# Mixture-of-experts stage: two experts share one picking matrix and one combination

## What is computed

```python
g_idx  = argmax(xf @ w_rg + b_rg)                 # one of 4 groups for each token
top_v, top_i = top_k(e_logits of that group, 2)   # two of its 8 experts
gates  = softmax(top_v) * g_gate
# each expert e works on the rows that chose it:
hdn = silu(x_e @ w1[e]) * (x_e @ w3[e])           # (rows, 1024) @ (1024, 512)
y_e = hdn @ w2[e]                                 # (rows, 512) @ (512, 1024)
out[token] = gates[token, 0] * y[slot 0] + gates[token, 1] * y[slot 1]
```

## Time and profile before

| | |
|---|---|
| Median of 3 executions | 1671.08 us (1670.26 to 1672.82) |
| The profiled execution | 1672.64 us |
| Its span, first to last instruction | 1670.8 us |
| Mean granted TensorE clock | 0.978 of 2.4 GHz |
| PE busy | 1581.0 us (95%) |
| First `hidden` of the MoE to the layer norm behind it | 178.1 to 635.8 us |

### The profile page before, as it was taken

The page is one execution under the profiler, slowest core; times in us unless marked ns, Lnnn a source line. Parts: engine busy times, 40 slices in busy tenths (PEclk is TensorE's granted clock), DMA queues, the critical chain, the costliest instruction groups (busy, mean ns, idle before and its releaser), DMA issues.

```text
span 1670.8 us, 20008 instructions
## 1 busy us (share of the span) xinstructions
PE 1581.0 (95%) x8054; PEld 1105.3 (66%) x8054; DVE 829.4 (50%) x1172; ACT 546.5 (33%) x717; POOL 61.3 (4%) x104
## 2 busy tenths in 40 slices
PE   8997999999999998999998899999999997899997
PEld 7744433333333336888897688888888886688886
DVE  1586311111111116655656766566655666576555
ACT  1251100000000003545444335444444534444442
POOL 2000000000000000000000000000000000000000
PEclk9997999999999999999989899999999998999999
DMA  9406899999999999853214359644755312179500
GB/s 312 143 1 251 349 413 429 428 428 428 428 430 428 428 407 348 277 181 125 76 51 152 123 198 367 212 132 151 264 196 169 101 59 93 51 262 353 191 0 26
DMA packets 149470, 395.20 MB, mean 237 GB/s; under 512 B 9458, under 2 KB 109936, under 8 KB 136608
## 3 DMA queue, kind: packets, MB, share of 16 engines
q1 hardware_dynamic: 146672, 385.67, 61.5%
q0 software_dynamic: 2736, 8.68, 1.4%
HBM read 393.28 MB, written 1.05 MB: 236 GB/s over the span
## 4 chain that ended last, share of the span: by engine, by line
PE 69%; DMA 15%; DVE 10%; issue 3%; ACT 3%; POOL 1%; SPq 0%; POOLq 0%; DVEq 0%; ACTq 0%
PE bank L1466 16%; DMA ring<-in_moe_w_dram 14%; PE bank L1494 12%; PE bank L1468 8%; PE bank L895 8%; PE bank L651 3%; PE bank L1481 3%; PE bank L924 2%; PE bank L704 2%; PE bank L1417 2%; PE bank L1510 1%; PE bank L912 1%; PE bank L2033 1%; PE bank L944 1%; DVE stats L546 1%
## 5 line engine op out<-in xcount | busy, mean ns | idle before, releaser
L895 PE MATMUL bank<-ring,arena 128*64 128x512 f32 x928 | 229.1, 596 | 9.8 <-DMA ring<-in_moe_w_dram 9.8
L1466 PE MATMUL bank<-x_both,split_u_hi 128*128 128x512 f32 x576 | 205.1, 399 | 0.0
L1466 PE MATMUL bank<-x_both,split_g_hi 128*128 128x512 f32 x576 | 205.0, 398 | 0.0
L895 PEld LDWEIGHTS bank<-ring,arena 128*64 128x64 f32 x928 | 68.0, 137 | 148.7 <-issue 116.0
L1468 PE MATMUL bank<-x_both,split_g_lo 128*128 128x256 f32 x576 | 161.7, 281 | 0.0
L1468 PE MATMUL bank<-x_both,split_u_lo 128*128 128x256 f32 x576 | 161.7, 281 | 0.0
L1125 DVE SCALAR_TENSOR_TENSOR arena<-arena,work 128x256 f32<-128x256 f32 x32 | 15.5, 485 | 288.8 <-PE bank L944 288.8
L1466 PEld LDWEIGHTS bank<-x_both,split_u_hi 128*128 128x128 f32 x576 | 108.2, 188 | 27.0 <-DVE split_u_lo L1283 0.3
L1466 PEld LDWEIGHTS bank<-x_both,split_g_hi 128*128 128x128 f32 x576 | 108.2, 188 | 26.4
L1283 DVE TENSOR_TENSOR split_d_lo<-ring,split_d_hi 128x2048 fp32r<-128x2048 f32 x40 | 91.7, 2292 | 58.1 <-ACT split_d_hi L1277 58.1
L1283 DVE TENSOR_TENSOR split_g_lo<-ring,split_g_hi 128x2048 fp32r<-128x2048 f32 x44 | 100.7, 2289 | 35.9 <-ACT split_g_hi L1277 35.9
(11 more groups left out here) (347 smaller groups left out, 2433.8 us busy)
## 6 DMA issues: line engine op xcount, KB each, us to landing
ring<-in_moe_w_dram SPq DMA_DIRECT2D x92, 2048.0 KB, 19.9
ring<-in_ffn_w_in_dram SPq DMA_DIRECT2D x88, 1024.0 KB, 9.3
ring<-in_ffn_w_out_dram SPq DMA_DIRECT2D x44, 1024.0 KB, 8.8
ring<-in_ml_w_in_dram SPq DMA_DIRECT2D x12, 1024.0 KB, 5.2
ring<-in_rec_w_in_dram SPq DMA_DIRECT2D x10, 1024.0 KB, 13.7
ring<-in_at_w_in_dram SPq DMA_DIRECT2D x6, 1024.0 KB, 5.2
ring<-in_rec_w_out_dram SPq DMA_DIRECT2D x5, 1024.0 KB, 9.9
gb_row<-in_ln_g_dram POOLq DMA_DIRECT2D x8, 512.0 KB, 7.0
```

What stands on the lines that cost most here:

```text
L895: i = nc.tensor.matmul(bank[4 + p][64 * j:64 * j + 64, :], xe[p][:, k, :], unit_view(n, 4)[:, k % 4, :], start=(k == 0), stop=(k == KT - 1))
L1466: nc.tensor.matmul(o[:], w_hi[:, at], x_both[:, k].rearrange("p a t -> p (a t)"), start=(k == 0), stop=False, skip_group_check=True)
```

## The change

The output rows of two experts are kept together: those of the even expert in partitions 0 to 63 of `y_2` (128 x 1024), those of the odd one in 64 to 127. `down(e)` therefore writes both halves j to partitions 64p to 64p + 63, half 0 in bank 5 and half 1 in bank 6. One picking matrix `pick_2` (128 slots x 128 tokens for each token tile) and one `combine(i)` serve experts 2i and 2i + 1; `combine` stands after the odd experts' `hidden`. `hidden` uses bank 4 for all experts. `keep` becomes two copies of 64 x 512. `down` waits for the copies of the expert before it. The second pass (overflow) is adapted in the same way, and SyncE waits for its end; that is not shown.

```diff
-        y_e = [arena[:, 9728 + i * 512:10240 + i * 512] for i in range(2)]
+        y_2 = arena[:, 9728:10752]
+        y_over = arena[:, 6144:7168]
...
+        place_2 = rt(968, NE // 2)
...
-                        i = nc.tensor.matmul(bank[4 + p][64 * j:64 * j + 64, :], xe[p][:, k, :], unit_view(n, 4)[:, k % 4, :],
+                        i = nc.tensor.matmul(bank[4][64 * j:64 * j + 64, :], xe[p][:, k, :], unit_view(n, 4)[:, k % 4, :],
...
                 pe.wait_ge(mo["hT"], e + 1)
+                if not (isinstance(e, int) and e == 0):
+                    pe.wait_ge(mo["ysb"], e)
...
-                        i = nc.tensor.matmul(bank[6][64 * j:64 * j + 64, :], hT_e[p][:, k, :],
+                        i = nc.tensor.matmul(bank[5 + j][64 * p:64 * p + 64, :], hT_e[p][:, k, :],
...
-            def combine(e, p, first=False, last=False):
+            def combine(i, first=False, last=False):
...
-                pe.wait_ge(mo["ysb"], e + 1)
-                pe.wait_ge(mo["sel"], e + 1)
+                pe.wait_ge(mo["ysb"], 2 * i + 2)
+                pe.wait_ge(mo["sel"], i + 1)
                 for t in range(TT):
                     for j in range(2):
-                        i = nc.tensor.matmul(bank[2 * t + j][:], pick_e[p][64 * j:64 * j + 64, t * P:(t + 1) * P],
-                                             y_e[p][64 * j:64 * j + 64, :], start=first, stop=last, skip_group_check=True)
+                        m = nc.tensor.matmul(bank[2 * t + j][:], pick_2[:, t * P:(t + 1) * P], y_2[:, j * HALF:(j + 1) * HALF],
+                                             start=first, stop=last, skip_group_check=True)
...
                     hidden(e, 1, 16 * (base + 2))
-                if e >= 2:
-                    combine(e - 2, e % 2, first=(e == 2))
+                    combine(0, first=True)
...
             with pe.Fori(2, NE // 2 - 1) as it:
                 for p in range(2):
                     hidden(2 * it + p, p, 16 * (it + base + p))
-                    combine(2 * it + p - 2, p)
+                    if p == 1:
+                        combine(it - 1)
                     down(2 * it + p - 1, 1 - p, 16 * (it + base + p))
                     turn(2 * it + p, p)
             hidden(NE - 2, 0, 16 * (base + NE // 2 - 1))
-            combine(NE - 4, 0)
             down(NE - 3, 1, 16 * (base + NE // 2 - 1))
             turn(NE - 2, 0)
             hidden(NE - 1, 1, 16 * (base + NE // 2), (0,))
-            combine(NE - 3, 1)
+            combine(NE // 2 - 2)
             down(NE - 2, 0, 16 * (base + NE // 2))
             hidden(NE - 1, 1, 16 * (base + NE // 2), (1,))
-            combine(NE - 2, 0)
             turn(NE - 1, 1)
             down(NE - 1, 1, 16 * (base + NE // 2))
...
-            combine(NE - 1, 1, last=True)
+            combine(NE // 2 - 1, last=True)
...
+            for p in range(2):
+                own.did(nc.vector.tensor_copy(place_2[64 * p:64 * p + 64, :], place[64 * p:64 * p + 64, 0, p::2]))
...
+            def pair_select(i, first=False):
                 if not first:
-                    dve.wait_ge(mo["comb"], e - 1)
-                select(e, p)
-                dve.wait_ge(own_sel, 2 * e + 2)
-                select_sum(p, mo["sel"])
+                    dve.wait_ge(mo["comb"], i)
+                select(pick_2, place_2[:, i:i + 1] if first else place_2[:, bass.ds(i, 1)])
+                dve.wait_ge(own_sel, 2 * i + 2)
+                nc.vector.tensor_tensor(pick_2, pick_2, sel_tmp, ALU.add).then_inc(mo["sel"], 1)
...
             with dve.Fori(1, NE // 2) as it:
                 for p in range(2):
                     expert(2 * it + p, p)
+                pair_select(it)
...
+            def keep(e, p, pair):
+
                 act.wait_ge(mo["y"], e + 1)
-                if not first:
-                    act.wait_ge(mo["comb"], e - 1)
-                nc.scalar.activation(y_e[p], bank[6][:], ACT.Copy).then_inc(mo["ysb"], 1)
+                if not (isinstance(pair, int) and pair == 0):
+                    act.wait_ge(mo["comb"], pair)
+                rows = slice(64 * p, 64 * p + 64)
+                nc.scalar.activation(y_2[rows, 0:HALF], bank[5][rows, :], ACT.Copy)
+                nc.scalar.activation(y_2[rows, HALF:], bank[6][rows, :], ACT.Copy).then_inc(mo["ysb"], 1)
```

More of the change, by code:

```diff
@@ L203, in build @@
         hT_e = [arena[:, 9216 + i * 256:9472 + i * 256].rearrange("p (k c) -> p k c", k=4) for i in range(2)]
-        y_e = [arena[:, 9728 + i * 512:10240 + i * 512] for i in range(2)]
+        y_2 = arena[:, 9728:10752]
+        y_over = arena[:, 6144:7168]
         rows_b = arena[:, 10752:11776].rearrange("p (v t) -> p v t", v=4)
         rows_diag = arena[:, 8192:9216].rearrange("p (v t j) -> p v t j", v=4, t=TT)
-        pick_e = [arena[:, 11776 + i * 256:12032 + i * 256] for i in range(2)]
+        pick_2, pick_over = [arena[:, 11776 + i * 256:12032 + i * 256] for i in range(2)]
         route_w = sb("route_w", [P, KT, NG + NE])
@@ L476, in overflow_loads @@
                     sp.dma_start(unit_view(j, kn), src).then_inc(ov["load"], 16)
+            sp.wait_ge(ov["y"], (BLOCKS - 1) * NE + 1)
         def pool_program(pool):
@@ L911, in early_hidden @@
                         w = unit_view(n, 4) if e < 2 else spare_view(j, k // 4)
-                        i = nc.tensor.matmul(bank[4 + p][64 * j:64 * j + 64, :], xe[p][:, k, :], w[:, k % 4, :],
+                        i = nc.tensor.matmul(bank[4][64 * j:64 * j + 64, :], xe[p][:, k, :], w[:, k % 4, :],
                                              start=(k == 0), stop=(k == KT - 1))
@@ L984, in moe_pe @@
                 pe.sem_inc(ov["comb"], 1)
+                pe.wait_ge(mo["ysb"], NE)
                 for n, b, e in each_overflow(pe):
@@ L999, in moe_pe @@
                         for j in range(2):
-                            i = nc.tensor.matmul(bank[6][64 * j:64 * j + 64, :], hT_e[0][:, k, :],
+                            i = nc.tensor.matmul(bank[5 + j][0:64, :], hT_e[0][:, k, :],
                                                  unit_view(4 + k // 2, 2)[:, k % 2, j * HALF:(j + 1) * HALF],
@@ L1007, in moe_pe @@
                         for j in range(2):
-                            i = nc.tensor.matmul(bank[2 * t + j][:], pick_e[0][64 * j:64 * j + 64, t * P:(t + 1) * P],
-                                                 y_e[0][64 * j:64 * j + 64, :], start=False, stop=False, skip_group_check=True)
+                            i = nc.tensor.matmul(bank[2 * t + j][:], pick_over[0:64, t * P:(t + 1) * P],
+                                                 y_over[0:64, j * HALF:(j + 1) * HALF], start=False, stop=False, skip_group_check=True)
                     i.then_inc(ov["comb"], 1)
-            combine(NE - 1, 1, last=True)
+            combine(NE // 2 - 1, last=True)
         def moe_dve(dve, own):
@@ L1119, in moe_dve, with select @@
                 th(nc.vector.tensor_scalar(place[:, b, :], place[:, b, :], -1.0, None, ALU.add))
+            for p in range(2):
+                own.did(nc.vector.tensor_copy(place_2[64 * p:64 * p + 64, :], place[64 * p:64 * p + 64, 0, p::2]))
+            dve.wait_ge(own_dve, own.n)
             dve.wait_ge(mo["rows_sb"], 2)
-            def select(e, p):
-                at_e = place[:, 0, e:e + 1] if isinstance(e, int) else place[:, 0, bass.ds(e, 1)]
-                nc.vector.scalar_tensor_tensor(out=pick_e[p], in0=rows_b[:, 0, :], scalar=at_e, in1=rows_b[:, 2, :],
+            def select(to, at):
+                nc.vector.scalar_tensor_tensor(out=to, in0=rows_b[:, 0, :], scalar=at, in1=rows_b[:, 2, :],
@@ L1133, in expert @@
-            def expert(e, p, first=False):
+            def pair_select(i, first=False):
                 if not first:
-                    dve.wait_ge(mo["comb"], e - 1)
-                select(e, p)
-                dve.wait_ge(own_sel, 2 * e + 2)
-                select_sum(p, mo["sel"])
+                    dve.wait_ge(mo["comb"], i)
+                select(pick_2, place_2[:, i:i + 1] if first else place_2[:, bass.ds(i, 1)])
+                dve.wait_ge(own_sel, 2 * i + 2)
+                nc.vector.tensor_tensor(pick_2, pick_2, sel_tmp, ALU.add).then_inc(mo["sel"], 1)
@@ L1139, in expert @@
+            def expert(e, p):
                 dve.wait_ge(mo["silu"], e + 1)
-                nc.vector.tensor_tensor(h_e[64:128, :], sil_e[64:128, :], bank[4 + p][64:128, :], ALU.mult).then_inc(mo["h"], 1)
+                nc.vector.tensor_tensor(h_e[64:128, :], sil_e[64:128, :], bank[4][64:128, :], ALU.mult).then_inc(mo["h"], 1)
                 dve.wait_ge(mo["tr"], e + 1)
                 nc.vector.tensor_copy(hT_e[p], bank[7][:].rearrange("p (k c) -> p k c", k=4)[:, :, C:]).then_inc(mo["hT"], 1)
-            expert(0, 0, True)
@@ L1145, in moe_dve @@
-            expert(1, 1, True)
+            expert(0, 0)
+            expert(1, 1)
+            pair_select(0, True)
             with dve.Fori(1, NE // 2) as it:
@@ L1148, in moe_dve @@
```

(39 more changed lines are left out.)

8 lines of the change are left out of this document (3 added, 5 removed).

## The result

The changed kernel takes 1744.47 us in the median (1743.38 to 1745.46, 4 runs), the kernel before 1670.67 (4 runs). The ratio is 1.0442, with a 95% interval of 1.0427 to 1.0457. That is 73.8 us slower; 1743.5 us was forecast.

A forecast was written before the change was run, and what follows sets the result against it. The prediction took expert weight transfers to bound the MoE, PE close behind, with the change moving the bound to PE. Its terms summed to +72.4 us, 1745.0 on the profiled execution, put at 1743.5 us, range 1732 to 1762.

The forecast's parts named there:

- What bounds it: MoE stage: expert weight transfers at 428 GB/s take 14.70 us per expert; PE needs 13.19, a slack of 1.5 us.
- down, +3.44 us each: Down's eight matmuls run one after the other, 6.88 us instead of 3.44, for each of 32 experts.
- the lone w1 matmul: First w1 matmul of hidden, running before w3 has landed: 1.07 us, two slots and a tail; nearest row for serial down.
- combine: Combination per pair: four whole-array matmuls, 3.44 us, plus 0.19 at the end; even expert loses 2.01 us, odd gains 1.72.
- Even experts' direct step to down: Even expert's hidden followed directly by down: 6.92 us to the next start instead of 7.02.
- The sum: Whole path: PE needs 32.97 us per pair, transfers 29.4, so the bound moves to PE; +72.4 us in total.
- 13 pairs: Experts 4 to 29: 13 pairs of 32.97 us, 428.6 us together; hidden(30) starts 64.2 us later than before.
- keep, +0.59 at the end: Two copies of 64 rows, 1.18 us for 0.60: hidden in the loop, 0.59 us on the path after expert 31.
- B: Rival: down's halves still share the array, being in different banks; a down under 5.2 us, 1671 us; chance 0.05.
- C: Rival: down's weight loads no longer overlap, 2.2 us a down, 70 us in all, 1814 us; chance 0.05.
- D: Rival: the clock falls as half the array idles; down at half speed costs 220 us more, 1960 us; chance 0.02.
- the strict theory of run 4: Matmuls enter the array in order, only neighbours on different halves share: down 6.5 to 7.0 us, 1738 to 1748 us.

The follow-up runs named there:

- run 1: Changed kernel with both halves of each down sent to different output partitions again, pairing kept: 1671.02 us, ratio 0.9993 to the kernel before.
- run 6: Changed kernel, its placement kept, with the downs of two experts issued together, matmul by matmul in turn, loads reordered: 1676.83 us, ratio 1.0041 to the kernel before.
- run 2: Changed kernel with only the odd experts' downs sending their halves to different output partitions again: 1689.83 us, ratio 1.0107 to the kernel before.
- run 3: Kernel before with only the placement changed, both halves of a down summed into the same 64 output partitions of one bank: 1748.43 us, ratio 1.0455.
- run 5: Kernel before with down's matmuls reordered: two of half 0, two of half 1, two of 0, two of 1: 1672.28 us, ratio 1.0014.
- run 4: Kernel before with down's matmuls reordered: four steps of half 0, then four of half 1: 1695.3 us, ratio 1.0135.

## Why the prediction was right

- **What bounds it.** Transfers at 428 GB/s with 1.5 us of PE's slack for each expert: runs 1 and 6 gave PE more slack and gained nothing, and run 2 used the slack up.
- **down, +3.44 us each.** Taken from the lone w1 matmul. Measured 6.96 and 7.02 us to the next start for 7.03; run 3 gives 7.02 with nothing else changed. This was the step on which all depended.
- **combine.** Forecast 3.63 us, measured 525.30 - 521.67 = 3.63. Even experts' direct step to down: 6.93 us against 6.92.
- **The sum.** Hidden(4) starts at 236.89 in the changed profile; forecast 234.9, with 2.0 us from before the stage, below. 13 pairs took 32.90 us each for 32.97. The last combination began at 707.82. Lines of the changed kernel's timeline of PE, from hidden(4) to the end of the stage:

```profile
236.89 1.51 PE L898 MATMUL bank<-ring,arena 128*64 128x512 f32 x6
...
664.59 7.09 PE L898 MATMUL bank<-ring,arena 128*64 128x512 f32 x32
...
699.57 7.08 PE L929 MATMUL bank<-ring,arena 128*64 128x512 f32 x16 [0.52 <-DVE arena L1147]
707.82 3.70 PE L949 MATMUL bank<-arena 128*128 128x512 f32 x8 [1.17 <-ACT arena L1190]
```

  The last combination starts 73.3 us after that of before, for 72.4 forecast. Of these, 2.1 us had come in before any changed instruction ran, so the stage itself added 71.2. The forecast was 1.2 us too high there, mainly the 0.07 us of each pair. That the total came within 1 us is partly luck: 2.1 us from outside the stage against 1.2 too much inside it.
- **keep, +0.59 at the end.** From the last down to the last combination 8.25 us for 4.35: +3.9, forecast 3.44 + 0.59.
- **The rivals.** B fell with the profile, a down of 7 us where B needs less than 5.2. Runs 1 and 3 show why: it takes other output partitions to share, other banks are neither needed nor enough. C fell with the profile, since 16 passes in 7.03 us leave no room for their loads. D fell with the stretch, whose granted clock is 1.00.
- The 2.1 us: PE's first projection (L651, now L654), untouched by the change, took 23.25 us in the changed kernel's profile and 20.99 in that of before. It comes with the execution and not with the change: run 5's profile has 20.99 too, and those of runs 3 and 4, whose first projection is also that of the kernel before, have 23.16 and 23.14. In run 1, where the transfers set the pace, the stage also began 2.1 us late and its last combination came only 0.2 us late; the changed kernel passes the delay on to its end. Its line in the changed kernel's timeline:

```profile
10.34 23.25 PE L654 MATMUL bank<-xT,ring 128*128 128x256 f32 x96 [0.78 <-DVE xT L779]
```

One thing the prediction left open: which of two matmuls on different halves may share. That it takes direct neighbours, as the strict theory of run 4 had it, is enough for the change, where no matmul of a down has one, but the array looks further, as runs 4 and 5 show.

## What to carry to other kernels

When a result is moved to other output partitions, ask which half of the array it now comes from, and what the matmul behind it uses: halves that alternate run at twice the rate here. PE's busy share (95% before and after), the number of records and their mean length don't tell the two apart; the busy time of their group does (116.9 and 225.8 us). Pairing two work items gave PE its lowest need, 25.68 us, only when their downs were issued in turn. And a saving is worth asking about only after the other limit has been read: here PE already has 3 us to spare for each pair of experts, and more of it gained nothing.

## What the runs showed of the hardware

- A float32 matmul of 128 x 64 by 512 columns holds its half of the array for two slots of 0.43 us. One for the other half starts early if at most one matmul that hasn't started stands ahead of it; with more, it waits (12 slots for fours, 8 for twos, 16 for eight on one half). This rule is read from these orders alone; whether the limit is one matmul or three records, and what it is for other shapes, stays open.
- The same look-ahead works across source lines. Behind down(30), on half 0, hidden's second part begins with a w1 matmul, also for half 0, and then a w3 matmul for half 1. In the changed kernel's timeline a record of hidden starts before the last record of that down. Half 0 is still taken, so I read it as the w3 matmul, which passes the w1 one:

```profile
692.44 0.64 PE L898 MATMUL bank<-ring,arena 128*64 128x512 f32 x1
692.86 0.59 PE L929 MATMUL bank<-ring,arena 128*64 128x512 f32 x1
```

- Spare time can lower the clock. In run 1 PE's waits came in one piece for each pair of experts. After the wait that ended at 468.21 the granted clock was at its lower level (0.50, 1.2 GHz) from 470 to 472 us, and the following hidden took 8.78 us instead of 7.08. Stretches and timeline of PE in run 1:

```profile
460.00:475.00 15.00, 12.75 (x50) 4.08 (x48) 1.12 (x2) 1.77 (x3) 0.61 (x1) 0.89 1.01 428
470.00:472.00 2.00, 2.00 (x8) 0.53 (x6) 0.00 (x0) 0.00 (x0) 0.00 (x0) 0.50 1.02 434
```

```profile
468.21 8.78 PE L898 MATMUL bank<-ring,arena 128*64 128x512 f32 x30 [2.25 <-DMA ring<-in_moe_w_dram]
497.57 7.08 PE L898 MATMUL bank<-ring,arena 128*64 128x512 f32 x30 [0.56 <-DMA ring<-in_moe_w_dram]
```

  It cost no time: the transfers set the pace, and PE's next wait was 1.69 us shorter, which is what the slow hidden had lost. The length of a wait alone doesn't settle it. Four of run 1's six waits of some 2.25 us were followed by such a slow hidden and two were not (that of experiment 1's timeline is one), and after run 6's 3.27 us down took its 7.09 us as ever.
